# An encoder layer on one core: the V projection of the first phase in 2x2 blocks with seven products

## The reference

```
def neighborhood_attention(x, w_qkv, rpb, w_o):        # x 1024 x 1024, w_qkv 1024 x 3072
    qkv = (x @ w_qkv).reshape(bsz, rows, GRID_W, 3, NA_HEADS, HEAD_DIM)
    q, k, v = qkv[:, :, :, 0] * HEAD_DIM ** -0.5, qkv[:, :, :, 1], qkv[:, :, :, 2]
    ...                                                  # windows of 8 x 16 tokens, bias, softmax, times v
    return out @ w_o
def reference(...):
    x = layer_norm(DN_ALPHA * x + neighborhood_attention(...), ln1_g, ln1_b)
    hid = jnp.square(jax.nn.relu(x @ w_ff1))
    ple = jax.nn.sigmoid(x @ w_ple_gate) * (p @ w_ple_proj)
    return layer_norm(DN_ALPHA * x + hid @ w_ff2 + ple, ln2_g, ln2_b)
```

## Time and profile before

| | us |
|---|---|
| median of 3 executions (lowest, highest) | 1223.27 (1221.71, 1224.21) |
| the profiled execution, its own time | 1221.3 |
| span of the profiled execution, first to last instruction | 1219.5 |
| PE busy in it | 1207.0 |
| DVE, ACT, POOL busy | 815.8, 588.0, 211.9 |

### The profile page before, as it was taken

How to read it: one execution, slowest core, us unless ns; L and a number is a source line. 1 busy time by engine, 2 the same in 40 slices (tenths; PEclk the granted TensorE clock), 3 DMA queues, 4 the chain that set the end, 5 groups by cost and what they waited for, 6 DMA issues and landing times.

```text
span 1219.5 us, 16871 instructions
## 1 busy us (share of the span) xinstructions
PE 1207.0 (99%) x5756; PEld 1012.8 (83%) x5756; DVE 815.8 (67%) x1586; ACT 588.0 (48%) x1139; POOL 211.9 (17%) x264
## 2 busy tenths in 40 slices
PE   9999999999999999999999999999999999999997
PEld 7887888888888888888888888888888888888886
DVE  3311666666667677769677677776764575588786
ACT  3311667677677633244444444444453433333571
POOL 0320555555554433200000000000000000000000
PEclk9999999999999999999999999999999999999999
DMA  8644333433244776683556556465579775778533
GB/s 259 203 127 123 92 94 76 125 111 117 85 121 146 247 221 201 191 312 113 176 211 240 189 208 229 171 239 192 205 250 379 282 271 215 262 242 307 190 104 104
DMA packets 166068, 232.57 MB, mean 191 GB/s; under 512 B 11872, under 2 KB 91872, under 8 KB 164576
## 3 DMA queue, kind: packets, MB, share of 16 engines
q1 hardware_dynamic: 165840, 231.37, 57.4%
q10 hardware_dynamic: 144, 0.13, 0.0%
HBM read 155.83 MB, written 67.29 MB: 183 GB/s over the span
## 4 chain that ended last, share of the span: by engine, by line
PE 96%; DVE 1%; DMA 1%; issue 1%; SPq 0%; ACT 0%; DVEq 0%; ACTq 0%
PE bank L2808 25%; PE bank L2776 25%; PE bank L1263 14%; PE bank L1403 7%; PE bank L1293 7%; PE bank L2732 6%; PE bank L1359 3%; PE bank L1338 3%; PE bank L1324 3%; PE bank L1396 1%; PE bank L1279 1%; PE bank L294 1%; DMA ple_embedding<-embedding_place 0%; DMA k_lo_twice<-k_lo_twice 0%; DMA x_chunk<-in_x 0%
## 5 line engine op out<-in xcount | busy, mean ns | idle before, releaser
L830 POOL TENSOR_TENSOR probabilities<-probabilities,total_reciprocal 128x384 f32<-128x384 f32 (+1 forms) x128 | 99.0, 774 | 153.7 <-DVE total_reciprocal L1148 153.5
L2776 PE MATMUL bank<-x_combination,weight_parts 128*128 128x512 f32 x504 | 118.5, 389 | 0.0
L963 ACT ACTIVATE probabilities<-negated_scores,negated_max 128x384 f32<-128x384 f32 (+1 forms) x128 | 75.5, 590 | 83.0 <-DVE negated_max L1142 82.9
L2776 PEld LDWEIGHTS bank<-x_combination,weight_parts 128*128 128x128 f32 x504 | 94.6, 188 | 19.6
L1263 PE MATMUL bank<-act_T_hi,w_qkv_hi 128*128 128x512 f32 x256 | 102.6, 401 | 0.0
L1263 PE MATMUL bank<-act_T_lo,w_qkv_hi 128*128 128x512 f32 x256 | 100.4, 392 | 0.0
L1263 PE MATMUL bank<-act_T_hi,w_qkv_lo 128*128 128x512 f32 x256 | 100.4, 392 | 0.0
L1142 DVE CUSTOM_DVE_ANT_0 negated_scores<-bank,bias_inner 128x384 f32<-128x384 f32 x96 | 53.2, 554 | 46.5 <-issue 46.0
L2776 PE MATMUL bank<-act_T_hi,weight_parts 128*128 128x512 f32 x240 | 77.3, 389 | 0.0
L2134 ACT ACTIVATE hidden_staging<-hidden_staging 128x512 f32<-128x512 f32 x48 | 30.3, 632 | 94.9 <-DVE hidden_staging L2474 94.9
L2808 PE MATMUL bank<-x_combination,hidden_parts_odd 128*128 128x512 f32 (+1 forms) x324 | 73.1, 381 | 0.0
(11 more groups left out here) (244 smaller groups left out, 2906.8 us busy)
## 6 DMA issues: line engine op xcount, KB each, us to landing
hidden_combinations<-hidden_staging SPq DMA_DIRECT2D x112, 256.0 KB, 2.2
w_ff_in<-in_w_ff SPq DMA_DIRECT2D x27, 1024.0 KB, 7.9
weight_raw<-in_w_ff SPq DMA_DIRECT2D x25, 1024.0 KB, 5.6
weight_raw<-hidden_combinations SPq DMA_DIRECT2D x14, 1024.0 KB, 5.5
hidden_in<-hidden_combinations SPq DMA_DIRECT2D x14, 1024.0 KB, 5.5
v_parts<-v_tile_parts SPq DMA_DIRECT2D x16, 512.0 KB, 3.8
weight_raw<-in_na_w_qkv SPq DMA_DIRECT2D x16, 512.0 KB, 3.8
v_hi_lo<-v_parts SPq DMA_DIRECT2D x8, 1024.0 KB, 5.6
```

The source lines that it names most:

```text
L830: nc.gpsimd.tensor_tensor(prob[:, u % 4, 0:n], prob[:, u % 4, 0:n], recip[:, u % 4:u % 4 + 1].to_broadcast([P, n]), ALU.mult).then_inc(pro ...
L963: nc.scalar.activation(prob[:, u % 4, 0:n], score[:, u % 2, 0:n], ACT.Exp, scale=-1.0, bias=nmax[:, u % 4:u % 4 + 1], accum_out=total[:, u ...
L2776: mm = nc.tensor.matmul(bank, w1_part(wp, u, p)[:, k, :], x_part(ap, p, k), start=(k == 0 and n == 0 and p in (1, 5, 6)), stop=(k == KH4 - ...
```

## The change

V is made by blocks. Call the two halves of the tokens (in window order) and of K the rows and columns of x, so that x = [[X11, X12], [X21, X22]] in 512x512 blocks, and the V weights likewise W = [[W11, W12], [W21, W22]]. In place of eight block products seven are made (`V_PRODUCTS = (1, 2, 5, 6, 7, 3, 4)`), each 4 banks x 4 chunks x 3 passes = 48 matmuls:

- 1: X11 W11 and 2: X12 W21. They are made chunk by chunk as x arrives, in the same four banks. Product 1 is copied to SBUF by ACT before 2 is added to it; the sum 1 + 2 in the bank is the first V block.
- 5, 6, 7 and 4 have a sum of x blocks as one operand, 5, 6, 7 and 3 a sum of weight blocks as the other; 4 has W22 as it is. Products 6, 7, 4 share the banks of 1 and 2: 7 and 4 are added onto what stands there ("one sum kept in PSUM"), after DVE has subtracted product 1 from 6 (`v_total`). Product 3 is added onto 5 in its bank.
- The sums of x: DVE makes the first and third (`x_sum_first`, `x_sum_third`, 128x256 pieces out of the turning banks, two of each kind per chunk), out of raw copies that ACT now makes of each turned chunk (`x_raw_copy`); POOL makes the second and fourth (`x_sums_second_fourth`, 8 subtractions of 128x512). Each is then split by ACT and DVE.
- The sums of weights are made by transfers that POOL issues, `dma_start(..., accum_op=ALU.add)`: a block of 128x4x512 float32 (1 MB) is read from memory and added to what lies in SBUF. There are seven; each waits for the one before it (`w_added`). Products 5, 6, 7 and 3 wait for the second, third, fifth and seventh of them. `wait_ge(w_added, ...)` of ACT stands ahead of the split of the sum, L1130 in the changed kernel.
- K of the first pair for both halves of the tokens is made chunk by chunk beside products 1 and 2 (`first_project`, from the third part of chunk 1 on, one chunk behind), and Q for the first half after them: 72 matmuls. They go to `first_k` and `first_q` in memory and come back by 8 loads (`load_first`). Between V and the first step only 12 matmuls are left. POOL's splits of the right half of V's weights are gone; `x_places` are four, so a chunk's place is reused.

The core of the diff:

```diff
-V_HALVES = 2
-V_TILES = V_HALVES * GROUPS
-FIRST_TILES = 6
+V_PRODUCTS = (1, 2, 5, 6, 7, 3, 4)
+V_SUMS = (5, 6, 7, 4)
+V_BLOCKS = ((0, 0), (1, 1), (0, 1), (1, 0))
+QUARTER = GROUPS // 2
+AHEAD_GROUPS = ((K_, 0, 2), (K_, 1, 3), (Q_, 0, 0))
+AHEAD_PRODUCTS = GROUP_MMS * len(AHEAD_GROUPS)
...
# POOL
+            def add_w_block(place, row, c, nth):
+                if nth:
+                    pool.wait_ge(w_added, 16 * nth)
+                nc.gpsimd.dma_start(place[:, :, :], w_block(row, c), accum_op=ALU.add).then_inc(w_added, 16)
+            x_sums_second_fourth(0)
+            pool.wait_ge(first_lo, w_parts(1, KC2 - 1))
+            add_w_block(w_sum2[0], 0, 1, 0)
+            x_sums_second_fourth(1)
+            pool.wait_ge(s1_sum, 16)
+            add_w_block(w_sum1[0], 1, 1, 1)
+            x_sums_second_fourth(2)
+            add_w_block(w_sum2[0], 1, 1, 2)
+            x_sums_second_fourth(3)
+            pool.wait_ge(w_first_in, 32)
+            add_w_block(w_sum4[0], 0, 1, 3)
+            pool.wait_ge(chunk_in[0], 64)
+            add_w_block(w_sum3[0], 0, 1, 4)
+            add_w_block(w_sum4[0], 1, 1, 5)
+            add_w_block(w_sum4[0], 0, 0, 6)
...
# ACT; W_SUM_1 .. W_SUM_4 are w_added at 32, 48, 80 and 112
+            def w_v_high(p, k):
+                if p in (1, 2):
+                    ...
+                else:
+                    act.wait_ge(*{5: W_SUM_1, 6: W_SUM_2, 7: W_SUM_3, 3: W_SUM_4, 4: W_22}[p])
+                if V_PRODUCTS.index(p) >= 2:
+                    act.wait_ge(v_full, v_done(V_PRODUCTS[V_PRODUCTS.index(p) - 2], QUARTER - 1))
+                nc.scalar.activation(w_high(p)[:, k, :], w_raw[p][:, k, :], ACT.Copy, scale=-1.0 if p == 3 else 1.0)
...
# PE
-            for n in range(FIRST_TILES, V_TILES):
-                v_tile(n)
-            project(0, AHEAD)
+            for k in range(KC):
+                passes = [(0,), (2,), (1,)] if k else [(0,), (1,), (2,)]
+                for n in passes:
+                    for i in range(QUARTER):
+                        first_products(1 + k // KC2, i, k % KC2, n)
+                    if n == passes[1] and k < KC - 1:
+                        for half in range(2):
+                            turn_x(k + 1, half)
+                for behind in {0: (), 2: (), KC2 - 1: (1, 2)}.get(k, (k - 1,)):
+                    for e in range(2):
+                        first_project(e, behind)
+            for e in range(2):
+                first_project(e, KC - 1)
+            for k in range(KC):
+                first_project(2, k)
+            for p in V_PRODUCTS[2:]:
+                v_product(p)
+            pe.wait_ge(v_lo, 2 * QUARTER + 1)
+            project(AHEAD_PRODUCTS, AHEAD)
```

More of the change, by code:

```diff
@@ L857, in _ @@
                 copy_bias(h)
+            for i in range(W_LOWS):
+                split(Q_, 0, i)
             for g in range(-UNITS, 0):
@@ new lines, in _ @@
+            for i in range(W_HIGHS):
+                first_w_high(Q_, i)
+            x_sum_high(5, KC2 - 1)
+            w_v_high(5, 0)
+            first_evac(0)
+            w_v_high(5, 1)
+            first_evac(1)
+            for k in range(2, KC2):
+                w_v_high(5, k)
+            first_evac(2)
+            for k in range(KC2):
+                w_v_high(6, k)
+                x_sum_high(6, k)
+                v_high(k)
+            for i in range(QUARTER):
+                v_copy(5, i)
@@ new lines, in _ @@
+            for k in range(KC2):
+                w_v_high(7, k)
+                x_sum_high(7, k)
+            for i in range(QUARTER):
+                v_copy(6, i)
+            for k in range(KC2):
+                w_v_high(3, k)
+            for k in range(KC2):
+                x_sum_high(4, k)
+            for k in range(KC2):
+                w_v_high(4, k)
+            for n in range(QUARTER, 2 * QUARTER + 2):
+                v_high(n)
+            for i in range(W_HIGHS):
+                split(Q_, 0, i)
@@ new lines, in first_evac @@
+            def first_evac(e):
+                kind, _, bank = AHEAD_GROUPS[e]
+                hi, low = (kq_place[e][:, part, :] for part in range(2))
+                dve.wait_ge(proj_hi, 2 * (e + 1))
+                if kind == Q_:
+                    last = nc.vector.scalar_tensor_tensor(out=low, in0=S.ps[bank][:, :], scalar=Q_SCALE, in1=hi.bitcast(F32),
+                                                          op0=ALU.mult, op1=ALU.subtract)
+                else:
+                    last = nc.vector.tensor_tensor(low, S.ps[bank][:, :], hi.bitcast(F32), ALU.subtract)
+                last.then_inc(proj_free, 2)
@@ new lines, in v_products @@
+            def v_products(p, i, k, passes=(0, 1, 2)):
+                bank = v_first_bank(i) if p in (1, 2, 6, 7, 4) else v_second_bank(i)
+                for n in passes:
+                    wp, ap = PASSES[n]
+                    mm = nc.tensor.matmul(bank, x_part[p](ap, k)[:, i * P:(i + 1) * P], (w_high(p), w_low[p])[wp][:, k, :],
+                                          start=(p in (1, 6, 5) and k == 0 and n == 0), stop=(k == KC2 - 1 and n == passes[-1]),
+                                          skip_group_check=True)
+                if k == KC2 - 1 and (1 in passes if p in (1, 2) else True):
+                    mm.then_inc(v_full, 1)
@@ new lines, in first_project @@
+            def first_project(e, k):
+                kind, t, bank = AHEAD_GROUPS[e]
+                if e == 2 and k == 0:
+                    pe.wait_ge(x3_sum, X_SUMS_3)
+                pe.wait_ge(first_lo, first_w_parts(kind, k // KC2))
+                for n, (wp, ap) in enumerate(PASSES):
+                    mm = nc.tensor.matmul(S.ps[bank][:, :], (w_kq_hi[kind], w_kq[kind][1])[wp][:, k, :],
+                                          S.act[ap][:, k, t * HALF:(t + 1) * HALF],
+                                          start=(k == 0 and n == 0), stop=(k == KC - 1 and n == 2))
+                if k == KC - 1:
+                    mm.then_inc(proj_full, 1)
```

615 lines of the change are left out of this document (432 added, 183 removed).

## The result

| | before | changed |
|---|---|---|
| median, us (lowest, highest; 4 runs each) | 1223.74 (1221.71, 1224.93) | 1234.34 (1232.08, 1234.5) |
| profiled execution, span | 1219.5 | 1232.5 |
| first score matmul of the attention starts at | 120.06 | 132.67 |

The ratio is 1.0084, with a 95% interval of 1.0066 to 1.0102. The first score comes 12.6 us later, the span is 13.0 us longer: the loss lies before the attention. The page answers to the earlier trace rows as follows.

A forecast was written before the change was run, and what follows sets the result against it. PE, busy nearly throughout, was taken as the bound, so time follows matmul count. Terms -10.9 + 3.1 + 0.5 + 0.6 = -6.7 us took the profiled 1221.3 to 1214.6, median 1216.6; range 1213 to 1231, likeliest case 1213 to 1220.

The forecast's parts named there:

- rival 2: Series of weight-sum transfers delays product 3: L = 9.2 gives +2.4 us, L = 10 gives +8, 1231; chance 0.23.
- Work removed: PE matmuls for V: 384 fall to 336, 48 fewer at 0.2268 us each, -10.9 us.
- Arrival of x: Chunk phase before product 5: matmuls wait for ACT and DVE pieces, +3.1 us, bounds 1 and 7.
- The weight sums by DMA: Seven accumulating transfers in a row: product 3 waits for the last, +0.5 us; called the main unknown.
- L: Time from issue of one accumulating transfer to issue of the next; taken as 7.9 us, bounds 5.6 and 11.2.
- Handing over: Banks passed between products, with copies by DVE and ACT, said to fit ACT narrowly: +0.6 us, bounds 0 and 3.
- V's last tiles need 4 x 0.69 us: End of V, before attention: DVE takes out the last four tiles while only 12 matmuls (2.7 us) give cover.
- Clock: First attention pair: a lower granted clock after a PE wait, named as something that would make the forecast wrong.
- Rival 3: Gain and loss meet: L between 8.2 and 8.8 or start 4 us worse, -2.4 to +2.4 us, 1223; chance 0.12.
- rival 1: Clean start (+1 us) and hidden weight-sum transfers, L under 7.8: -9.9 us, 1213.4; chance 0.15.

The follow-up runs named there:

- e2: Changed kernel with the same seven GpSimd transfers as plain overwriting loads, without the add (weight sums wrong); 1219.46 us, 0.9974 of the kernel before.
- e12: Changed kernel with only those accumulating transfers that add to the same place waiting for each other, others side by side; 1227.58 us, 1.0037 of the kernel before.
- e1: Changed kernel with the seven accumulating transfers left out, so weight blocks are not summed; 1217.34 us, 0.996 of the kernel before.
- e8: e1 with the Q weights loaded early and split while product 4 runs; 1221.0 us, 0.9977 of the kernel before.
- e10: e9 and e11 together; 1215.48 us, 0.9938 of the kernel before.
- e11: Changed kernel with V tiles 4 to 7 taken out and stored earlier, 8 to 11 out earlier, Q weights early in their own place; 1238.06 us, 1.0115.
- e4: Changed kernel with GpSimd issuing the first accumulating transfer ahead of its subtractions of x; 1228.21 us, 1.0042 of the kernel before.
- e6: Changed kernel with five of the seven accumulating transfers replaced by eight additions on GpSimd; 1224.48 us, 1.0008 of the kernel before.
- e7: e6 with the Q weights loaded early and split while product 4 runs; 1227.67 us, 1.0041 of the kernel before.
- e9: e6 with its eight additions made by VectorE instead of GpSimd; 1219.39 us, 0.9971 of the kernel before.

## Why the prediction was wrong

The forecast was 1216.6 us and faster; the second rival, that the chain decides, was put at 2.4 to 8 us slower, 1231. It took place, and went 3 us beyond its far end.

- **Work removed, -10.9:** right. 48 fewer matmuls, still 0.227 us apart.
- **Arrival of x, +3.1:** somewhat too high. The first matmul starts at 6.51 (predicted 6.5), the next four at 7.99 (7.8), chunk 1 at 11.60 (11.75). Behind chunk 4 the order was kinder: turning 5 starts at 28.9 where I had 30.4. Product 5 starts at 53.34 (54.9). The sum also took 1.03 us for each turning where the earlier trace rows shows 0.87 to 0.88 from piece to piece: in the kernel before, turnings and idle time up to the end of V are 6.9 us, not 7.6. Against that the term is 2.3.
- **The weight sums by DMA, +0.5:** this is the step that failed. I took L = 7.9, the row of a load issued by SP beside other traffic, for an operation that the trace did not have. It is 9.3 without much traffic and 10.0 on average; rival 2's 9.2, worked out as a double moved part, was right for the undisturbed ones. With L = 10 rival 2 had product 3 wait 15.2 us. Its operands came at 102.3, 16.3 us after it was due by the measured start of product 5, and it started 16.7 us late: that mechanism was right, though PE spent the time in stops ahead of it. The Trainium skill's sentence on two source reads (Collectives: The Full Stack, Part 3), which I named and did not follow, is about reduce-scatter in a ring. That an add is slower agrees with 9.3 against 5.95 in e2; that two reads are the reason no run shows. The rest of the step is what I left out: I asked of each sum only whether it was in time for its product, not what the transfers do to the stores of K, Q and V, which free places, nor what stands behind a waiting split. Product 6 waited for slowed stores even when its sum was early (e12), and product 7 not for its operand but for the copy of product 6 behind the splits. While the chain ends at 100.9 this costs PE only 0.4 us more; in e12, where product 3's operands were there at 92.6, it started 2.7 us later. What the term measured, clock included, is 17.0 us (e1).
- **Handing over, +0.6:** the four handings over fit when nothing is late: in e1 none waits. In the changed kernel they are the place where the late third sum is felt.
- **"V's last tiles need 4 x 0.69 us", with 12 matmuls as cover:** wrong. I costed the taking out but not the four places, each free only when a store is done. The stores of the last twelve tiles are mostly issued four together and take 3.2 to 9.1 us; in e1, without adds, 3.3 to 11.5, so for these it is not the adds (for the first four it is, 7.8 against 3.0). That it is their bunching and the 2.5 MB of K and Q beside them is my reading; no run separated these. With the Q weights, landed 9.5 us after their issue at 115.1, this is a 3.7 us wait and 1.6 us of clock. e8 and e10 point to two bounds here of nearly equal height.
- **Clock, 0:** named as a risk for the first pair and not costed. It was 6.1 us, about a third of the difference.
- **Rival 3's condition** does not fit its own time: by the sum, -2.4 to +2.4 us belongs to L from 8.4 to 9.2, not 8.2 to 8.8. Nothing else hangs on it.

The account closes. Of the 22.2 us lost from product 5 to the first score, 1.1 were in the sum for chain and handing over; the stop ahead of the first score, 0.9 from start to start, is gone; and the arrival was better by 0.8. That leaves 19.4. By the sum the first score was due at 113.4, and it came 19.3 later. The span is 19.7 above the sum.

Without these two errors the sum would have been near: e1, with neither chain nor sums, took 1217.3 and still had 3.2 us of wait and 1.6 us of clock. Taken off, that is 1212.5 for the clean scheme, where rival 1 gave 1213.4. But this is a subtraction. e8 took the wait away and another came, 1221.0; e10, with 2.6 us of waits left, is the nearest that a run came. e10, which computes all of it, is 1.1 us under the forecast; that it comes near is owed to a repair, not to the step being right.

That half clock is a cost of its own is read from rows; no run changed it alone. That the loads of K and Q are what the first score of e11 waits for is argued from their start times only.

## What to carry to other kernels

Where a chain needs an operation that no row shows, take it from the far bound until it is measured, and first ask whether sums can be built on one another, so that fewer transfers are needed. A stop of PE that names something else can lie ahead of a bound that a late chain sets anyway: compare the time at which the chain's last operand is ready with the start of the product that uses it. Nor is a transfer priced by its own product alone: ask which stores it slows, and list what stands behind the waiting instruction on its engine, above all work that frees banks or places. A wait that is removed shows the next one; at a place where two bounds are equally high, either change alone gives nothing or less than nothing.

## What the runs showed of the hardware

- An accumulating transfer of 1 MB issued by GpSimd takes 9.3 us from issue to the next, 9.8 to 13.6 beside other traffic; the same without the add 5.95 to 6.2, and beside other traffic 7.9 to 9.8 from issue to landing (e2). It holds GpSimd 1.3 us, the plain one 0.77. Two at once took 8.4 to 10.4 us each at first and up to 16.3 later, where V stores ran too (e12).
- A VectorE subtraction of 128x512 takes 0.68 us, and 1.2 to 1.8 while GpSimd works on SBUF too, if both its operands are in SBUF.
- PE's granted clock fell to half at the end of single waits or behind them, for 3.4, 6.8 or 10.2 us: 3.4 at 2.0 us in e4, at 3.2 in e1 and at 3.9 in e6; at 5.3 us 6.8 in e7 and 10.2 in e8. A wait of 2.0 us in the changed kernel, and one of 3.45 in e9 at the same place as in e1, left it at the upper level. So the length of a wait alone does not tell what it costs.
- The 512 KB stores of V took 6.9 to 9.3 us (medians of the kernels here), 3.8 in the kernel before. Of those, the ones issued alone in the kernel before took 2.7 to 4.1 us; the first four in e1, issued 1.8 us apart with no accumulating transfer beside them, 2.8 to 3.8, and with such transfers 7.1 to 8.7 (the changed kernel).
